# Second block of a transformer kernel: projections from a token-major x that is not yet normed, root and shift applied behind the product

## The chip, the cores and the metric

The kernel runs on one core of a Trainium2 chip. The metric is the device time of the whole program in microseconds, the median of three runs. The engines are named as in the profile: PE is the matmul engine (PEld its weight load), DVE the vector engine, ACT the scalar engine, POOL GpSimd, SP the engine that issues the weight loads.

## The reference

256 tokens of width 1024 go through a first block of two layers (sparse attention, short convolution, gated mix, MLP) and then through a second block, which the change is about:

```python
x = rmsnorm(x, norm_final)                       # end of the first block
ada = silu(c) @ w_ada + b_ada                    # shift1, scale1, gate1, ...
h = rms_norm(x, norm1_g) * (1 + scale1) + shift1
qa, ka, va, qb, kb, vb = split(h @ w_in)         # 512, 128, 128, 512, 512, 512 columns
o_a = windowed_gqa(qa, ka, va)                   # 8 heads, bias and sink
o_b = neighbourhood_attention(qb, kb, vb)        # 8 heads, bias
x = x + gate1 * (concat(rms_norm(o_a), rms_norm(o_b)) @ w_out)
x = x + gate2 * peer(rms_norm(x, norm2_g) * (1 + scale2) + shift2)
return rms_norm(x, final_g)
```

## The kernel before

**Pieces.** All weights come as one stream of 544 pieces of 128 x 1024 floats into a ring of four slots. Each piece is split into a high part (ACT, `split_hi`, L185) and the rest (DVE, `split_lo`, L190), and each product is three matmuls (`mm3`, L213 to L215: high by high, high by low, low by high). `next_piece` (L197) issues the split of the piece three ahead and then makes PE wait for the split of its own. `piece_b` (L217) turns one piece into one tile of 128 outputs by 256 tokens with 24 matmuls of 256 columns. `piece_a` (L242) has the activations as the standing operand, with 12 matmuls of 512 columns per piece.

**Queues.** Every engine works through its instructions in the order in which the Python text issues them. `VE.go`, `AC.go` and `PE.done` (L79 to L90) tie them with semaphores. An instruction that waits holds up all behind it on its engine. Line L88 in the profile is the helper that records nearly all DVE and ACT operations of the two attention blocks.

**The seam into the second block.** The last MLP of the first block ends with three `down` pieces that are held back (`held_pieces`, L337): for each of the four accumulator banks (two token tiles by two halves of the width) all three pieces run in a row, so that the banks end one after another. Behind each, `sum_of` (L1198) adds the bank to x, multiplies by the final gain into `xn`, and ACT takes squares of both. After the last bank PE runs 25 filling matmuls (`keep_clock`, L1221), while DVE makes sums, mean and root (`root`, L292) and two diagonal matrices that hold each token's root. Then `modulated_to_u` (L1153) multiplies `xn` by the diagonals on PE (L1169), which turns it to feature-major and scales it at once; ACT and DVE add scale and shift and split it into `u_hi` and `u_lo`.

**The projections.** `project` (L1374) is a generator of 18 steps over 18 pieces: ka and the first qa tile together (`two_pieces`, L229), the other qa tiles, va, then kb and qb in turn, four times, and last vb, whose four pieces use `piece_a` and so come out token-major. Everything is evicted by ACT alone (`evicted`, L1369). The loop at L1446 runs the steps, and a table written by hand, `beside`, says which attention units take one step behind which projection step. A unit (`unit`, L1254) is one token tile of one attention: a generator whose steps are scores of heads on PE with their bias added on DVE (two steps, the second ends with a maximum over the row on DVE), exponentials on ACT (two steps of four heads), transposes of the probabilities (two steps, evicted by ACT and DVE), the product with v, the scaling by the branch's gain, the transposes into `mx_hi` and `mx_lo`. Units a0 and a1 are the windowed attention, b0 and b1 the neighbourhood one. `masked` (a mask added to the bias of b, steps 0 to 3), `root(st2, ...)` (step 4) and `own_scale` (the norm that x itself gets, steps 5 and 6) are DVE work put between.

Of the kernel before, what the change touches and what calls it, by code (L numbers as in the profile page):

```python
# [49 lines left out]
U_SHIFT, U_REST = 56, 8  # L50
# [43 lines left out]
def build(nc, stream, x_in, gains2, gain_cols, conv_w, w_ada, b_ada, c_cols, kept_in, rope_in, na_mask_in,  # L94
          t5_in, t5_hot, rpb_pad, sinks, sub_keys, gain_out, out):
    ctx = ExitStack()
    with ctx:
# [17 lines left out]
        u_hi = sb(ctx, "u_hi", [P, KD, T], F32R)  # L115
        u_lo = sb(ctx, "u_lo", [P, KD, T], F32R)
# [100 lines left out]
        def piece_b(o, rhs_hi, rhs_lo, kt=KD, parts=1, last=False, ready=None):  # L217

            s = next_piece(last)
            for part in range(parts):  # L220
                for k in range(kt):
# [3 lines left out]
                    i = mm3(o[part], w_hi[:, s, col:col + P], w_lo[:, s, col:col + P],  # L225
                            rhs_hi[:, k, :], rhs_lo[:, k, :], k == 0, k == kt - 1)
            return used(i)
# [288 lines left out]
        gcol = sb(ph1, "gcol", [P, 2, KD])  # L516
# [134 lines left out]
        for layer in range(LAYERS):  # L651
# [409 lines left out]
            if layer < LAYERS - 1:  # L1061
                down(1, tile0 + KH - 3, False)
# [5 lines left out]
            last_tiles = [(a_hi, a_lo, 1), (o_hi, o_lo, 0), (o_hi, o_lo, 1)]  # L1068
            if layer < LAYERS - 1:
                last_tiles.pop(0)  # L1070
            last_downs = (len(last_tiles), lambda j, tt: [a[:, last_tiles[j][2], tt * P:(tt + 1) * P] for a in last_tiles[j][0:2]],
                          acc)
# [20 lines left out]
        og, junk = sb(ph1b, "og", [P, 2, W]), sb(ph1b, "junk", [P, 2, W])  # L1093

# [57 lines left out]

        def modulated_to_u(src, marks, scaled, j, on_act):  # L1153
# [40 lines left out]
        space_lo = [space[:, 0, 0:512], space[:, 2, 0:512]]  # L1194
        scaled = column_scale(0, ada_norm1)
        x_marks, g_marks = [[None, None], [None, None]], [[None, None], [None, None]]

        def sum_of(tt, n):  # L1198
            cols = slice(n * 512, (n + 1) * 512)
            x_marks[tt][n] = add_chunk(x, tt, n, mlp_scale)  # L1200
            g_marks[tt][n] = VE.go((x_marks[tt][n], (s_gain2, 32)), V.tensor_tensor, xn[:, tt, cols],
                                   x[:, tt, cols], gains_b[:, 0, cols], ALU.mult)

        def sums():
            for tt in range(NT):
                for n in range(2):
                    sum_of(tt, n)
                    square_of(x, 5, x_marks, tt, n)
                    if tt + n < NT:
                        square_of(xn, 7, g_marks, tt, n)  # L1210
                    yield

        def square_of(src, row, marks, tt, n):
            cols = slice(n * 512, (n + 1) * 512)
            junk_mark[0] = AC.go((marks[tt][n], junk_mark[0]), S.activation, space_lo[0], src[:, tt, cols], ACT.Square,
                                 accum_out=st[:, row + n, tt:tt + 1])
            return junk_mark[0]

        splits = held_pieces(*last_downs, sums())
        take(5)  # L1220
        keep_clock(5, 25)  # L1221
        m = VE.go((g_marks[1][1],), V.scalar_tensor_tensor, space_lo[1], xn[:, 1, 512:], 1.0, xn[:, 1, 512:],
                  ALU.mult, ALU.mult, accum_out=st[:, 8, 1:2])
        VE.wait(m, junk_mark[0])
        m1 = VE.go((m,), V.tensor_tensor, st[:, 0, :], st[:, 5, :], st[:, 6, :], ALU.add)
        m = VE.go((m,), V.tensor_tensor, st[:, 9, :], st[:, 7, :], st[:, 8, :], ALU.add)
        m1 = VE.go((m1,), V.tensor_scalar, st2[:, 1, :], st[:, 0, :], 1.0 / D, EPS, ALU.mult, ALU.add)
# [854 lines left out]
```

## Time and profile before

| what | value |
|---|---|
| runs | 1728.52 us median of 3 (1727.76 to 1728.98) |
| profiled execution | 1727.02 us, its span 1725.7 us |
| PE, PEld busy | 1700.7 us (99%), 1567.1 us (91%) |
| DVE, ACT busy | 1328.3 us (77%), 926.5 us (54%) |
| granted PE clock | 0.997 over the span |
| weight stream | 544 loads of 512 KB, 3.3 us from issue to landing |

A busy PE in this table is a PE with a matmul in its pipeline; the modelled length of one matmul overlaps the next, so the distance between starts says more than the busy time. Times in the timelines are microseconds from the start of the span, and a row with xN merges N instructions in a row.

### The profile page before, as it was taken

How to read it: one execution, taken by the hardware profiler on the slowest of the kernel's cores; microseconds unless marked ns; L12 is line 12 of the kernel's file. 1: busy time of each engine (PE TensorE's matmuls, PEld its weight loads, DVE VectorE, ACT ScalarE, POOL GpSimd, SP SyncE). 2: the span in 40 equal slices, each digit the busy share in tenths (PEclk: the TensorE clock that was granted, in tenths of full speed). 3: DMA queues.
4: the chain of work that ended last, by engine and by line, in shares of the span. 5: the costliest groups of instructions: out<-in, count | busy, mean ns of one | idle time of the engine just before them, and what ended most of it. 6: DMA issues, size and time to landing. Idle time of an engine off the chain costs nothing.

```text
span 1725.7 us, 33390 instructions
## 1 busy us (share of the span) xinstructions
PE 1700.7 (99%) x11670; PEld 1567.1 (91%) x11670; DVE 1328.3 (77%) x2382; ACT 926.5 (54%) x1647; POOL 63.3 (4%) x112
## 2 busy tenths in 40 slices
PE   9999999999999999999999999999999999999997
PEld 8899899989999899999889999999999988888886
DVE  7986778778976788877775999978888766666666
ACT  5454544455454544455554555577777655444553
POOL 0000001000000122100000000000000000000000
PEclk9999999999999999999999999999999999999999
DMA  6555687755445699744344555554444455555554
GB/s 233 174 187 205 209 294 270 250 174 171 159 160 168 221 329 327 238 153 140 123 167 152 173 170 179 182 171 141 141 138 144 141 191 193 194 194 194 191 192 152
DMA packets 90122, 327.30 MB, mean 190 GB/s; under 512 B 11000, under 2 KB 11176, under 8 KB 89584
## 3 DMA queue, kind: packets, MB, share of 16 engines
q1 hardware_dynamic: 79056, 286.45, 48.8%
q0 software_dynamic: 9712, 34.36, 6.0%
q10 hardware_dynamic: 1264, 5.24, 0.8%
q8 instruction: 62, 1.02, 0.2%
q14 instruction: 28, 0.23, 0.0%
HBM read 323.88 MB, written 6.09 MB: 191 GB/s over the span
## 4 chain that ended last, share of the span: by engine, by line
PE 80%; DVE 16%; issue 2%; ACT 1%; DMA 0%; DVEq 0%; ACTq 0%
PE bank L213 24%; PE bank L215 24%; PE bank L214 24%; DVE Z L88 6%; DVE w_lo L190 5%; PE bank L1772 3%; PE bank L284 1%; DVE yc L88 1%; PE bank L276 1%; PE bank L1313 1%; PE bank L484 1%; DVE work L88 1%; DVE rot L88 1%; DVE top L88 1%; PE bank L1264 0%
## 5 line engine op out<-in xcount | busy, mean ns | idle before, releaser
L190 DVE TENSOR_TENSOR w_lo<-raw,w_hi 128x1024 fp32r<-128x1024 f32 x544 | 658.0, 1220 | 154.1 <-ACT w_hi L185 153.3
L185 ACT ACTIVATE w_hi<-raw 128x1024 fp32r<-128x1024 f32 x544 | 572.5, 1054 | 229.2 <-PE bank L215 162.4
L213 PE MATMUL bank<-u_hi,w_hi 128*128 128x256 f32 x2400 | 686.2, 286 | 3.7 <-DVE w_lo L190 3.0
L214 PE MATMUL bank<-u_lo,w_hi 128*128 128x256 f32 x2400 | 674.7, 281 | 0.0
L215 PE MATMUL bank<-u_hi,w_lo 128*128 128x256 f32 x2400 | 674.7, 281 | 0.0
L213 PEld LDWEIGHTS bank<-u_hi,w_hi 128*128 128x128 f32 x2400 | 453.0, 189 | 12.8 <-DVE w_lo L190 4.3
L214 PEld LDWEIGHTS bank<-u_lo,w_hi 128*128 128x128 f32 x2400 | 453.2, 189 | 2.3
L215 PEld LDWEIGHTS bank<-u_hi,w_lo 128*128 128x128 f32 x2400 | 452.9, 189 | 0.0
L215 PE MATMUL bank<-w_hi,a_lo 128*128 128x512 f32 x744 | 290.6, 391 | 0.0
L214 PE MATMUL bank<-w_lo,a_hi 128*128 128x512 f32 x744 | 290.4, 390 | 0.0
L213 PE MATMUL bank<-w_hi,a_hi 128*128 128x512 f32 x744 | 289.9, 390 | 0.0
L215 PEld LDWEIGHTS bank<-w_hi,a_lo 128*128 128x128 f32 x744 | 139.6, 188 | 29.4
L213 PEld LDWEIGHTS bank<-w_hi,a_hi 128*128 128x128 f32 x744 | 139.9, 188 | 27.9 <-issue 0.2
L214 PEld LDWEIGHTS bank<-w_lo,a_hi 128*128 128x128 f32 x744 | 139.6, 188 | 28.1
L1861 ACT ACTIVATE a_hi<-Z 128x256 fp32r (+1 forms) x126 | 52.7, 418 | 169.0 <-PE bank L215 167.2
L1863 DVE TENSOR_TENSOR a_lo<-Z,a_hi 128x256 fp32r<-128x256 f32 x126 | 53.6, 425 | 81.6 <-ACT a_hi L1861 81.6
L1761 ACT ACTIVATE rows_a<-rows_a,sel 128x128 f32<-128x128 f32 x256 | 81.2, 391 | 0.0
L1745 DVE TENSOR_TENSOR rows_a<-kept,sel 128x512 f32<-128x512 f32 x64 | 44.2, 691 | 34.5 <-PE bank L1772 34.5
L962 ACT ACTIVATE qT<-bank 128x256 f32<-128x256 f32 x64 | 24.6, 384 | 82.5 <-PE bank L215 82.3
L1608 ACT ACTIVATE Z<-bank 128x256 f32 (+1 forms) x68 | 26.1, 384 | 76.8 <-PE bank L215 76.7
L971 DVE CAST a_hi<-qT 128x256 fp32r<-128x256 f32 x60 | 18.1, 301 | 48.4 <-PE bank L215 47.3
L997 DVE SCALAR_TENSOR_TENSOR space<-gate,c_tmp,space 128x1024 f32 x42 | 53.7, 1280 | 0.4
(286 smaller groups left out, 1710.6 us busy)
## 6 DMA issues: line engine op xcount, KB each, us to landing
raw<-stream SPq DMA_DIRECT2D x544, 512.0 KB, 3.3
gate<-w_ada POOLq DMA_DIRECT2D x48, 512.0 KB, 6.0
t_rows<-t_by_distance POOLq DMA_DIRECT2D x8, 256.0 KB, 3.1
rpb_rows<-rpb_pad POOLq DMA_DIRECT2D x8, 224.0 KB, 4.1
bias_b<-rpb_rows POOLq DMA_DIRECT2D x16, 96.0 KB, 6.3
bias_a<-t_rows POOLq DMA_DIRECT2D x1, 1536.0 KB, 13.1
x<-x_in ACTq DMA_DIRECT2D x2, 512.0 KB, 5.5
gains_b<-gains POOLq DMA_DIRECT2D x1, 1024.0 KB, 8.7
```

The costliest lines, as they stand in the source:

```text
L88: return self.done(method(*args, **kw))
L185: nc.scalar.activation(w_hi[:, s, :], raw[:, s, :], ACT.Copy).then_inc(s_hi, 1)
L190: nc.vector.tensor_tensor(w_lo[:, s, :], raw[:, s, :], w_hi[:, s, :].bitcast(F32), ALU.subtract).then_inc(s_split, 1)
L213: M.matmul(o, lh, rh, start=start, stop=False, skip_group_check=True)
L214: M.matmul(o, lh, rl, start=False, stop=False, skip_group_check=True)
L215: return M.matmul(o, ll, rh, start=False, stop=stop, skip_group_check=True)
L997: nc.vector.scalar_tensor_tensor(total, ada_raw[:, k % ADA_RING, :], c_act[:, k:k + 1], total, ALU.mult, ALU.add).then_inc(s_ada, 1)
L1745: return V.tensor_tensor(out, iota.unsqueeze(1).to_broadcast([P, GROUP, P]), values.unsqueeze(2).to_broadcast([P, GROUP, P]), ALU.is_equal)
L1761: i = S.activation(rows_a[:, q, e, :], rows_a[:, q, e, :], ACT.Copy, scale=share[:, e:e + 1])
L1772: i = M.matmul(bank[6 + q][:, e * P:(e + 1) * P], rows_a[:, q, e, :], rows_b[q][:, e, :].bitcast(F32), start=True, stop=True, skip_group_c ...
L1861: S.activation(hi[:, q, :], zj, ACT.Copy).then_inc(s_ah, 1)
L1863: V.tensor_tensor(lo[:, q, :], zj, hi[:, q, :].bitcast(F32), ALU.subtract).then_inc(s_al, 1)
```

## The change

- The held `down` pieces of the last layer are two, as in the first layer; the third runs before them as a piece of its own.
- Behind them x is transposed as it is (16 transposes, two tiles of features to a bank, banks 4 to 7), and ACT and DVE scale it by one gain per feature, which now holds norm_final, norm1_g and 1 + scale1, and split it into u. No root is in it. The filling matmuls, `xn`, the diagonal product and `modulated_to_u` are gone here.
- u has 272 columns for each tile of features instead of 256. Columns 256 and 257 hold the shift, so each of the 18 products has 258 columns, and column 256 of the result is what the shift adds to that output.
- ACT squares x into buffers that are kept; DVE multiplies two tensors of these (four operations over 128x512) for the second mean; `two_roots` follows at step 1, and `roots_as_row` at step 4 makes a 128x256 tile with each token's root in its column.
- Each projection leaves its bank by `rooted_and_shifted`: ACT copies column 256, DVE multiplies the bank by the row of roots, ACT adds the copied column. The first three wait for the row and are issued at step 4, the next three at step 5.
- vb is projected feature-major as the rest and transposed afterwards (`turned_vb`, 8 transposes and two copies behind the first `w_out` piece).
- Units a0 and a1 begin at steps 5 and 6 instead of 3 and 4. `masked` moves to steps 8 to 11, `root(st2)` to step 10, `own_scale` to steps 14 and 15.

```diff
-U_SHIFT, U_REST = 56, 8
+U_SHIFT, U_REST = 8, 8
+U_WIDE = T + 16
...
-            last_tiles = [(a_hi, a_lo, 1), (o_hi, o_lo, 0), (o_hi, o_lo, 1)]
+            last_downs = (2, lambda j, tt: [a[:, j, tt * P:(tt + 1) * P] for a in (o_hi, o_lo)], acc)
...
+        LOWER_ORDER = (0, 2, 1, 3, 4, 6, 5, 7)
+        def lower_scaled(k, hi, lo, j, scaled, turned):
+            b, col = turn_place(k)
+            src, gain, t = bank[b][:, col:col + T], acol[:, 2 * j + 1, k:k + 1], turned[k | 1]
+            m1 = AC.go((t, scaled, *(free[b] if k % 2 else ())), S.activation, hi[:, k, 0:T], src, ACT.Copy, scale=gain)
+            m = VE.go((m1, t, scaled), V.scalar_tensor_tensor, lo[:, k, 0:T], src, gain, hi[:, k, 0:T].bitcast(F32),
+                      ALU.mult, ALU.subtract)
...
+        def roots_as_row(b):
+            take(b)
+            PE.wait(got["diag", 0], got["diag", 1])
+            for tt in range(NT):
+                i = M.matmul(bank[b][:, tt * P:(tt + 1) * P], one[:, 0:1].to_broadcast([P, P]), diag[:, tt, :],
+                             start=True, stop=True, skip_group_check=True)
+            m = AC.go((PE.done(i),), S.activation, token_row[:, :], bank[b][:, 0:T], ACT.Copy)
...
+        def rooted_and_shifted(b, dst, n, done, row):
+            m1 = AC.go((done,), S.activation, side_sum[:, n:n + 1], bank[b][:, T:T + 1], ACT.Copy)
+            m = VE.go((done, row, m1), V.tensor_tensor, dst, bank[b][:, 0:T], token_row[:, :], ALU.mult)
+            free[b] = (m, m1)
+            return AC.go((m, m1), S.activation, dst, dst, ACT.Identity, bias=side_sum[:, n:n + 1])
...
         splits = held_pieces(*last_downs, sums())
-        take(5)
-        keep_clock(5, 25)
...
-        diagonals(root(st, NT, m))
-        split_hi(splits[0]), split_hi(splits[1])
-        split_lo(splits[0])
-        h_ready = modulated_to_u(xn, g_marks, scaled, 0, 0)
-        split_lo(splits[1])
+        for k in range(4, KD):
+            turn_tile(k, 0, x_marks, turned)
+        for k in range(KD):
+            turn_tile(k, 1, x_marks, turned)
+        h_ready = {k: lower_scaled(k, wide_hi, wide_lo, 0, scaled, turned) for k in LOWER_ORDER}
+        for c in splits:
+            split(c)
+        squares_kept(1)
+        for tt in range(NT):
+            for n in range(2):
+                sq = squared[:, 2 * tt + n, :]
+                m = VE.go((square_marks[tt, n],), V.scalar_tensor_tensor, sq, sq, 1.0,
+                          gain_squares[:, n * 512:(n + 1) * 512], ALU.mult, ALU.mult,
+                          accum_out=st[:, 7 + n, tt:tt + 1])
...
         def project():
+            def product(b, ready=None):
+                take(b)
+                return piece_b([bank[b][:, 0:T + 2]], *RAW, ready=ready, order=LOWER_ORDER if ready else None)
+            PE.wait(*shifts)
+            first = [(0, kaT[:, :], "ka", product(0, h_ready))]
             yield
             for f in range(KW):
+                first.append((1 + f, qT[:, f, :], ("qa", f // 2 * 2), product(1 + f)))
+                if f == KW - 1:
+                    row = roots_as_row(7)
+                    for b, dst, name, m in first[0:3]:
+                        got[name] = rooted_and_shifted(b, dst, b, m, row)
+                yield
+            m = product(5)
+            for b, dst, name, done in (*first[3:], (5, vaT[:, :], "va", m)):
+                got[name] = rooted_and_shifted(b, dst, b, done, row)
             yield
+            for f in range(KW):
+                m = product(4)
+                got["kb", f] = rooted_and_shifted(4, kT[:, f, :], 6 + 2 * f, m, row)
+                yield
+                m = product(5)
+                got["qb", f] = rooted_and_shifted(5, qbT[:, f, :], 7 + 2 * f, m, row)
+                yield
+            for f in range(KW):
+                m = product(4 + f % 2)
+                got["vT"] = rooted_and_shifted(4 + f % 2, vT[:, f, :], 14 + f, m, row)
+                yield
...
-        beside = {3: (a0,), 4: (a1,), 5: (a0,), 6: (a1, a0), 7: (a0, a1), 8: (a1,), 9: (a0,),
+        beside = {5: (a0,), 6: (a1, a0), 7: (a0, a1), 8: (a0, a1), 9: (a1, a0),
                   10: (a1, a0), 11: (a1, a0), 12: (a1, b0), 13: (a0, a1), 14: (a0, a1, b0), 15: (b1, b0),
                   16: (b1,), 17: (b0, b1)}
         for n, _ in enumerate(main):
+            if n == 1:
+                mean_mark = two_roots(m)
             if n == 6:
                 turned_va()
-            if n < 4:
-                masked(n)
-            if n == 4:
+            if 8 <= n < 12:
+                masked(n - 8)
+            if n == 10:
                 r1_mark = root(st2, NT, mean_mark)
-            if n in (5, 6):
-                own_scale(n - 5, r1_mark)
+            if n in (14, 15):
+                own_scale(n - 14, r1_mark)
...
             used(i)
+            if k == 0:
+                turned_vb()
             for u in side:
                 next(u)
```

## Rows read from the trace of the kernel before

**Rows 1.** Part 4 of the page: the chain that ended last, shares of the span by engine.

```profile
PE 80%; DVE 16%; issue 2%; ACT 1%; DMA 0%; DVEq 0%; ACTq 0%
```

**Rows 2.** Windows: stretch, us; busy us of PE, PEld, DVE, ACT, POOL; granted clock; DMA.

```profile
775.00:801.00 26.00, 26.00 (x212) 23.98 (x211) 25.61 (x45) 13.11 (x33) 0.00 (x0) 1.00 0.45 146
...
801.00:842.00 41.00, 40.10 (x286) 34.88 (x285) 28.26 (x49) 20.86 (x47) 0.00 (x0) 1.00 0.37 127
```

**Rows 3.** Timeline of PE at the seam: start us, length us, engine, line, operation.

```profile
758.73 5.62 PE L276 MATMUL bank<-one_r 128*128 128x512 f32 x25
...
764.19 3.73 PE L1169 MATMUL bank<-space,xn 128*128 128x128 f32 x32
...
767.68 0.36 PE L213 MATMUL bank<-u_hi,w_hi 128*128 128x256 f32 x1
...
779.21 1.14 PE L1264 MATMUL bank<-kaT,qT 64*128 64x256 f32 x8
```

**Rows 4.** Timeline of PE at the seam between the two layers.

```profile
382.08 0.60 PE L366 MATMUL bank<-kept,x 128*128 128x128 f32 x4
...
383.91 1.77 PE L366 MATMUL bank<-kept,x 128*128 128x128 f32 x12
...
385.44 0.36 PE L213 MATMUL bank<-u_hi,w_hi 128*128 128x256 f32 x1
...
388.58 0.28 PE L213 MATMUL bank<-u_hi,w_hi 128*128 128x256 f32 x1
```

**Rows 5.** Timeline of DVE at the seam into the second MLP.

```profile
575.54 3.22 DVE L88 SCALAR_TENSOR_TENSOR u_lo<-bank,kept,u_hi 128x256 fp32r<-128x256 f32 x8
```

**Rows 6.** Timeline of DVE in the second block, and one row of its MLP.

```profile
760.43 0.69 DVE L88 SCALAR_TENSOR_TENSOR space<-xn 128x512 f32<-128x512 f32 x1
...
761.17 0.23 DVE L88 TENSOR_TENSOR st<-st 128x2 f32<-128x2 f32 x2
...
764.07 1.22 DVE L190 TENSOR_TENSOR w_lo<-raw,w_hi 128x1024 fp32r<-128x1024 f32 x1
...
777.32 1.21 DVE L190 TENSOR_TENSOR w_lo<-raw,w_hi 128x1024 fp32r<-128x1024 f32 x1
...
778.46 0.95 DVE L88 TENSOR_TENSOR bias_b<-bias_b,na_mask 128x768 f32<-128x768 f32 x1
...
781.33 1.28 DVE L88 SCALAR_TENSOR_TENSOR space<-bank,bias_a 128x512 f32<-128x512 f32 x2
...
790.21 2.29 DVE L88 TENSOR_REDUCE rows<-space 128x8 f32<-128x2048 f32 x1
...
793.02 1.22 DVE L190 TENSOR_TENSOR w_lo<-raw,w_hi 128x1024 fp32r<-128x1024 f32 x1
...
581.32 0.41 DVE L965 TENSOR_TENSOR qT<-qT,bank 128x256 f32<-128x256 f32 x1
```

**Rows 7.** Timeline of ACT in the second block.

```profile
769.75 0.42 ACT L88 ACTIVATE u_hi<-hT 128x256 fp32r<-128x256 f32 x1
...
792.93 0.51 ACT L88 ACTIVATE space<-space,rows 128x256 f32<-128x256 f32 x1 [4.08 <-DVE rows L88]
...
794.92 1.04 ACT L185 ACTIVATE w_hi<-raw 128x1024 fp32r<-128x1024 f32 x1
...
804.63 0.19 ACT L88 ACTIVATE rows<-rows 128x8 f32<-128x8 f32 x1
```

**Rows 8.** Timeline of PE in the second block, where the units' PE work begins.

```profile
801.43 1.03 PE L284 MATMUL bank<-kept,space 128*128 128x128 f32 x8
...
805.14 1.03 PE L284 MATMUL bank<-kept,p 128*128 128x128 f32 x8
...
815.38 0.37 PE L213 MATMUL bank<-u_hi,w_hi 128*128 128x256 f32 x1
...
845.38 1.09 PE L284 MATMUL bank<-kept,space 128*128 128x128 f32 x8 [0.34 <-ACT space L88]
...
852.78 1.04 PE L284 MATMUL bank<-kept,p 128*128 128x128 f32 x8
```

More of the change, by code:

```diff
@@ L215, in mm3, with piece_b @@
             return M.matmul(o, ll, rh, start=False, stop=stop, skip_group_check=True)
-        def piece_b(o, rhs_hi, rhs_lo, kt=KD, parts=1, last=False, ready=None):
+        def piece_b(o, rhs_hi, rhs_lo, kt=KD, parts=1, last=False, ready=None, order=None):
             s = next_piece(last)
+            order = order or tuple(range(kt))
             for part in range(parts):
-                for k in range(kt):
+                for k in order:
                     if ready is not None:
@@ L1204, in sums @@
-        def sums():
[L1205 to L1217, printed above, removed]
@@ new lines, in two_roots @@
+        def two_roots(m):
+            VE.wait(m, junk_mark[0])
+            m1 = VE.go((m,), V.tensor_tensor, st[:, 0, :], st[:, 5, :], st[:, 6, :], ALU.add)
+            m = VE.go((m,), V.tensor_tensor, st[:, 9, :], st[:, 7, :], st[:, 8, :], ALU.add)
+            m1 = VE.go((m1,), V.tensor_scalar, st2[:, 1, :], st[:, 0, :], 1.0 / D, EPS, ALU.mult, ALU.add)
+            m = VE.go((m,), V.tensor_scalar, st[:, 4, :], st[:, 9, :], 1.0 / D, None, ALU.mult)
+            m = VE.go((m, m1), V.scalar_tensor_tensor, st[:, 1, :], st2[:, 1, :], EPS, st[:, 4, :],
+                      ALU.mult, ALU.add)
+            diagonals(root(st, NT, m))
+            return m1
@@ new lines, in turned_va, with turned_vb @@
+            got["vat"] = free[7] = (m,)
+        vT = hT
+        def turned_vb():
+            marks = []
+            for tt in range(NT):
+                b = 4 + tt
+                take(b)
+                PE.wait(got["vT"])
+                for f in range(KW):
+                    i = M.transpose(bank[b][:, f * P:(f + 1) * P], vT[:, f, tt * P:(tt + 1) * P], ident)
+                i = PE.done(i)
+                if tt:
+                    m = VE.go((i,), V.tensor_copy, v_sb[:, tt, :], bank[b][:, :])
+                else:
+                    m = AC.go((i,), S.activation, v_sb[:, tt, :], bank[b][:, :], ACT.Copy)
+                free[b] = (m,)
+                marks.append(m)
+            got["vb"] = tuple(marks)
@@ L1399, in project @@
-                AC.go((m,), S.activation, kT[:, f, :], bank[b][:, 0:T], ACT.Copy)
-                m = AC.go((m,), S.activation, qbT[:, f, :], bank[b][:, T:2 * T], ACT.Copy)
-                free[b] = (m,)
-                got["qb", f] = m
-                yield
-            for g in range(KD // 2):
-                m = piece_a([[bank[4][:, :]], [bank[5][:, :]]], U, (2 * g, 2 * g + 1), 512,
-                            g == 0, g == KD // 2 - 1, (4, 5) if g == 0 else ())
-                if g < KD // 2 - 1:
-                    yield
```

119 lines of the change are left out of this document (57 added, 62 removed).

## The prediction

> **What bounds the kernel now.** I read the chain that ended last first: 80% of it is PE [rows 1], so a stage is worth what it adds to PE's own work plus what PE waits in it. Next the windows from 775 to 842 us: PE keeps a granted clock of 1.00, DVE is busy 25.61 us of 26.00 in the first and 28.26 of 41.00 in the second [rows 2]. DVE runs full while the projections start, and PE feels nothing of it, since splits are issued three pieces ahead. Then PE's timeline at the seam: 5.46 us of filling matmuls from 758.73 us, the diagonal product from 764.19, the first projection matmul at 767.68 [rows 3]. These 8.95 us are what the change is after. Last, the timelines of DVE and ACT, for prices and for the order of their queues [rows 6, 7], and the times at which PE begins the units' work [rows 8].
>
> **The seam.** The seam between the two layers has the new shape already: two held pieces, four transposes ahead of the last bank, twelve behind it. There the four take 0.35 us (382.08, next matmul 382.43), from 383.91 to the first product matmul 385.44 are 1.53 us, and the first product, fed by the lowering, lasts until 388.58, 3.14 us [rows 4]. The new code lowers tile 0 only when tile 1 is transposed, and behind four transposes of tiles 4 to 7: five transposes later, about 0.4 us. So: 758.73 + 0.35 + 1.53 + 0.4 = 761.05 for the first product, 764.2 for its end. Before, the pair began at 767.68, and four pieces of 24 matmuls ran to 779.21 [rows 3], 0.120 us each or, without the gaps between pieces, 0.1185 and 2.84 us a piece; half of the pair ends at 770.5. **Gain 6.3 us at the end of the first product.**
>
> **Small terms on PE.** Two columns more: 25 matmuls of 512 columns take 5.46 us, 0.218 each, those of 256 0.120 [rows 3], so 0.4 ns a column and 0.35 us for 18 x 24 x 2. The row of roots is two full matmuls of 128 columns; 32 records of the diagonal product take 3.49 us [rows 3], four records 0.45. vb by `piece_b` costs about what `piece_a` does, some 0.15 us for four. `turned_vb` is eight transposes, 0.9 us by 0.11 each (12 and the wait fit in 1.53 us [rows 4]). Together +1.85. If nothing waited, the change would give 6.3 - 1.85 = 4.4 us.
>
> **DVE at the start.** Its first lowering starts near 760.4 and eight take 3.22 us [rows 5], to 763.65. Then in the order of the queue: one split at 1.14 (777.32 to 778.46 [rows 6]), ready 765.05; four squares times squared gain at 0.74 (760.43 to 761.17), 768.0; two splits, 770.3; `two_roots` at 2.9 (761.17 to 764.07, the same operations), 773.2; three splits, 776.65. PE without a wait starts products 1 to 4 at 764.2, 767.1, 769.9 and 772.8 and wants the split of product 3 at 769.9, which is there at 769.15: it holds, with 0.8 us. Product 5 (va) starts behind the row, at 776.1. So far all gain is kept.
>
> **The new eviction.** It goes ACT, DVE, ACT, and ACT's next copy stands behind its last add, so a run of them does not overlap. Price of one: 0.19 us for a short ACT operation, 0.41 for a DVE product of 128x256 out of a bank, 0.42 for an ACT operation over 128x256 [rows 6, 7]: 1.0 us on ACT, of which DVE loses the same when it has nothing else ahead. Lower bound 0.4 (perfect overlap, DVE's part alone), upper bound 1.1 (the ACT operation at the 0.51 of an exponential with a bias [rows 7]); I take 1.0, since the code's order excludes the overlap. By "ScalarE: Activation LUTs" of the Trainium skill (section on what happens when an exp ACTIVATE runs) a per-partition bias adds about 93 ns to an ACTIVATE, which would put the last step near 0.49 us, the walk below some 0.9 us later and the sum at 1739.5. By that rule; the exponential with its bias, 0.51 us over the same 256 elements [rows 7], agrees.
>
> **What queues behind it.** The three evictions of step 4 run on ACT from 776.7 to 779.75. The first unit's scores need them: PE waits 0.9 us at 779. ACT's `split_hi` (1.0, 794.92 [rows 7]) and DVE's split follow, to 781.95, and only then the evictions of step 5, of which the second frees bank 4 at 783.4. kb0 needs bank 4, and PE, done at 780.9, waits 2.5 us more. From 784.3 DVE has the two units' scores and maxima: 1.20 for two heads' pairs (781.33, length 1.28), 2.81 for a maximum with its small operations (790.21 to 793.02), 1.14 a split [rows 6], without a hole until about 799.9. ACT makes the second half of a0's exponentials (2.0 us for four, 792.93 to 794.92 [rows 7]) only behind the eviction of step 8, which waits for DVE's product there, which stands behind a1's maximum and a split. That gives 800.3 + 2.0 = 802.3. PE, at step 9, is there at 798.25 and **waits 4.1 us**; its transposes began at 801.43 before [rows 8], so here the gain is gone (+1.0). a1 is worse: first half to 804.4, `split_hi` to 805.4, DVE's split and product to 806.95, ACT's add to 807.35, second half to 809.4. PE asks at 806.05, waits 3.4 us, and begins a1's transposes at 809.5 against 805.14 [rows 8], +4.4. Step 10 puts a split, a product, a mask (0.95, 778.46 [rows 6]) and the root (an estimate of 1.7: `two_roots` less its sums and diagonals) ahead of the copies that PE's next transposes want, and the first qb piece behind a0's product with v starts at 819.8 against 815.38 [rows 8], still +4.4.
>
> **The second half.** From step 13 DVE has again no hole: the branch's scales 2.0 (a root and its small operations, an estimate from `two_roots`), two og 1.3 and later two mx_lo 1.2 (512 elements each, like the squares' 0.69), a split, a product, `own_scale` 1.2 (1024 elements like a split), scores 1.2 and b0's maximum 2.2 (2.29 at 790.21 [rows 6]), the last done near 841.65. Against before this stretch holds six evictions and two `own_scale` more. PE waits 0.8 us for og, 2.5 us for a bank that b1's first scores hold, and 1.6 us for the last vb tile, then transposes it (0.95). b0's second exponentials stand behind that tile's eviction, and its transposes start at 855.6 against 845.38; b1's at 862.9 against 852.78 [rows 8]: **+10.1 us**. Behind this everything has the old order and the old load, and the shift goes through to the end.
>
> **Sum.** 1727.0 + 10.1 = 1737.1 against the profiled execution, whose time lies 1.5 us under the median; so 1738.6. All other edits I count at nothing: shift columns, squared gains (1.2 us of DVE ahead of the held pieces, beside a piece that PE runs for 2.8 us) and the wider u. `u_hi` and its neighbours move in memory; no row tells a price for that, and no row of before differs between tiles of u, so zero.
>
> **The rivals.** (1) **PE stays the bound.** All waits of the walk close up, because the exponentials come before PE asks. Then -4.4 us: 1724.1. For it: DVE's and ACT's work sums to less than the stage (DVE is idle for 12.7 us of 41 from 801 us on [rows 2]). Against: it would need both units' exponentials 4 us earlier than the queues give. This is the side other than my forecast, and the point where it decides is step 9: exponentials of a0 ready before 798 us. 0.14. (2) **The evictions cost DVE only 0.4 us each.** The first half then comes some 4 to 5 us earlier and meets PE with little loss; the second half, which is DVE's plain sum, still adds 5 to 6. +5: 1733.5. 0.18. (3) **The clock falls.** The waits of 3 to 4 us are the first of this length; before, filling matmuls stood in the one gap that was longer, and the clock was 1.00 throughout [rows 2]. At 1.2 GHz a piece of 2.84 us takes 5.7; twice this, half of it hidden in the next wait, is about +3: 1741.6. 0.12. "TensorE: Matmul & The Clock Gate" of the Trainium skill (Part 1, the clock gate) says that an array left idle is throttled to half its clock until it has been busy again; whether these waits are enough no row here shows. (4) The terms cancel: gain at the seam, waits of 4 to 5 us, nothing to see. 0.08.
>
> **The numbers.** The forecast has 0.48. 0.2% is 3.5 us, about what a measurement of this kernel tells from no change. Slower by more: forecast, most of (2), and (3), 0.74. Within: (4) and the fast edge of (2), 0.12. Faster: (1), 0.14. The range runs from the fast rival to the slow one with the bounds of the eviction: 1723.5 to 1743.0. The likeliest case's own range is 1735 to 1742.
>
> **What would show it.** Right: first projection matmul near 761 us; a wait of PE for bank 4 at step 6; transposes of L284 behind a wait for ACT at steps 9 and 10, each 3 to 4 us; DVE busy above 85% from 784 to 853; b0's transposes near 855.6. Wrong: transposes of a0 at 798 without a wait, and w_out pieces starting before 842.08; then (1). A first product later than 762 would show that the seam was misread. A granted clock under 1.00 behind the waits would be (3).

## The result and the profile after

| | before | after |
|---|---|---|
| median of the runs | 1728.75 us (4 runs) | 1759.8 us (4 runs) |
| ratio | | 1.0181 [1.0169, 1.0194] |
| profiled span | 1725.7 us | 1759.0 us |
| granted PE clock over the span | 0.997 | 0.992 |

Slower, as forecast, but by 31 us in place of some 10, and outside the range. The chain that ended last is mostly PE's as before ([rows 1]); PE's share fell from 80% to 78%, and those of DVE and ACT each grew by one point:

```profile
PE 78%; DVE 17%; issue 2%; ACT 2%; DMA 0%; DVEq 0%; ACTq 0%
```

The same windows as [rows 2], then the long one that the prediction names (DVE above 85%), then five short ones. The columns are as there; the figure behind POOL is the granted clock.

```profile
775.00:801.00 26.00, 22.45 (x169) 20.79 (x168) 19.02 (x42) 9.39 (x21) 0.00 (x0) 0.93 0.41 139
801.00:842.00 41.00, 33.59 (x266) 31.95 (x264) 27.53 (x67) 22.41 (x63) 0.00 (x0) 0.96 0.27 91
784.00:853.00 69.00, 56.64 (x427) 52.24 (x428) 50.69 (x98) 32.99 (x89) 0.00 (x0) 0.95 0.26 88
788.00:792.00 4.00, 3.58 (x17) 3.58 (x18) 2.97 (x5) 2.02 (x4) 0.00 (x0) 0.57 0.41 135
806.00:812.00 6.00, 2.54 (x12) 2.55 (x13) 2.13 (x5) 5.07 (x19) 0.00 (x0) 0.75 0.27 87
850.00:856.00 6.00, 4.34 (x20) 3.24 (x20) 4.90 (x8) 3.51 (x12) 0.00 (x0) 0.78 0.26 87
856.00:862.00 6.00, 6.00 (x30) 5.72 (x30) 4.97 (x5) 2.21 (x5) 0.00 (x0) 0.65 0.28 92
862.00:875.00 13.00, 10.41 (x49) 8.47 (x48) 5.19 (x7) 9.73 (x29) 0.00 (x0) 0.87 0.33 120
```

PE loses 3.55 us of the first window and 7.41 of the second, DVE is less busy than before in the first (19.02 against 25.61), and the clock, 1.00 before, falls to 0.57 in one stretch. From 784 to 853 us DVE is busy 50.69 of 69 us, 73%. No engine is full: this is a stage of engines that wait for each other.

Timeline of PE in the changed kernel. L1161 transposes x, L215 to L217 are the three matmuls of a product, L1331 scores, L287 the units' transposes. In brackets stands the idle time ahead of a row and who ended it.

```profile
762.75 0.39 PE L217 MATMUL bank<-w_hi,o_lo 128*128 128x512 f32 x1
762.98 1.66 PE L1161 MATMUL bank<-kept,x 128*128 128x128 f32 x12
764.97 0.36 PE L215 MATMUL bank<-u_hi,w_hi 128*128 128x258 f32 x1 [0.33 <-DVE u_lo L89]
...
784.84 1.14 PE L1331 MATMUL bank<-kaT,qT 64*128 64x256 f32 x8 [1.12 <-ACT qT L89]
788.42 0.49 PE L215 MATMUL bank<-u_hi,w_hi 128*128 128x258 f32 x1 [2.44 <-DVE qT L89]
...
789.14 0.42 PE L215 MATMUL bank<-u_hi,w_hi 128*128 128x258 f32 x1
789.35 0.42 PE L216 MATMUL bank<-u_lo,w_hi 128*128 128x258 f32 x1
...
809.46 1.97 PE L287 MATMUL bank<-kept,space 128*128 128x128 f32 x8 [3.99 <-ACT space L89]
...
816.58 1.10 PE L287 MATMUL bank<-kept,p 128*128 128x128 f32 x8 [1.76 <-ACT p L89]
...
852.73 2.64 PE L1331 MATMUL bank<-kT,qbT 64*128 64x256 f32 x8 [1.66 <-DVE p L89]
...
867.32 1.12 PE L287 MATMUL bank<-kept,space 128*128 128x128 f32 x4 [2.59 <-ACT v_sb L89]
...
875.72 1.04 PE L287 MATMUL bank<-kept,p 128*128 128x128 f32 x8
...
909.00 0.36 PE L215 MATMUL bank<-u_hi,w_hi 128*128 128x256 f32 x1
```

Three landmarks cut the program: the start of the last held `down` matmul (758.49 us before, 762.75 here), the first product matmul behind the attention block (886.04, 909.00) and the end of the span.

| part | before | after | more |
|---|---|---|---|
| up to the last held matmul | 758.49 | 762.75 | 4.3 |
| attention stage | 127.55 | 146.25 | 18.7 |
| all behind it | 839.66 | 849.99 | 10.3 |

The last part runs no instruction that the change rewrites, and the first only a few at its end, but both are longer. In the last part the same matmuls start a little farther apart. PE in the last phase, first before, then after:

```profile
1500.03 0.39 PE L213 MATMUL bank<-w_hi,a_hi 128*128 128x512 f32 x1
...
1502.75 0.39 PE L213 MATMUL bank<-w_hi,a_hi 128*128 128x512 f32 x1
```

```profile
1500.09 0.39 PE L215 MATMUL bank<-w_hi,a_hi 128*128 128x512 f32 x1
...
1502.89 0.39 PE L215 MATMUL bank<-w_hi,a_hi 128*128 128x512 f32 x1
```

Twelve matmuls of the same size take 2.72 us in one and 2.80 in the other; the length shown for one is 0.39 in these rows, so only the starts tell it. The distance from the start of one matmul to the start of the next is called the step below. Its means over 1400 to 1700 us are 0.2267 and 0.2333 us. Behind the stage stand 3 x 504 such matmuls: 1512 x 0.0066 = 10.0 of the 10.3 us. The first part is less certain: kernels with the same instructions and the same layout up to there (s_dve_moved and s_dve_moved_bank6, below) reach that landmark at 758.07 and 761.00 us, so differences of up to 3 us between single profiles mean little there.

### The profile page after: what moved, and what is told of

The parts are those of the page before. It is cut to its first block, busy times and chain, and to the rows that moved or that the text cites. A ratio compares the mean times of both kernels' runs of the same rounds, so it can differ in the third digit from the quotient of the medians.

```text
span 1759.0 us, 33500 instructions
## 1 busy us (share of the span) xinstructions
PE 1721.9 (98%) x11689; PEld 1577.9 (90%) x11689; DVE 1335.1 (76%) x2402; ACT 930.0 (53%) x1662; POOL 63.5 (4%) x112
## 4 chain that ended last, share of the span: by engine, by line
PE 78%; DVE 17%; issue 2%; ACT 2%; DMA 0%; DVEq 0%; ACTq 0%
PE bank L215 24%; PE bank L217 23%; PE bank L216 23%; DVE Z L89 6%; DVE w_lo L192 5%; PE bank L1847 3%; DVE yc L89 1%; PE bank L1380 1%; PE bank L287 1%; PE bank L487 1%; DVE work L89 1%; DVE rot L89 1%; PE bank L279 1%; DVE top L89 1%; DVE rows L89 0%
## 5 line engine op out<-in xcount | busy, mean ns | idle before, releaser
L215 PE MATMUL bank<-u_hi,w_hi 128*128 128x256 f32 (+1 forms) x2432 | 699.3, 288 | 5.3 <-DVE qT L89 2.4
L216 PE MATMUL bank<-u_lo,w_hi 128*128 128x256 f32 (+1 forms) x2432 | 687.8, 283 | 0.0
L217 PE MATMUL bank<-u_hi,w_lo 128*128 128x256 f32 (+1 forms) x2432 | 684.8, 282 | 0.0
L215 PEld LDWEIGHTS bank<-u_hi,w_hi 128*128 128x128 f32 x2432 | 460.4, 189 | 16.2 <-issue 4.3
L216 PEld LDWEIGHTS bank<-u_lo,w_hi 128*128 128x128 f32 x2432 | 461.4, 190 | 2.8
L217 PEld LDWEIGHTS bank<-u_hi,w_lo 128*128 128x128 f32 x2432 | 463.5, 191 | 0.0
L217 PE MATMUL bank<-w_hi,a_lo 128*128 128x512 f32 x744 | 294.1, 395 | 0.0
L215 PE MATMUL bank<-w_hi,a_hi 128*128 128x512 f32 x744 | 293.8, 395 | 0.0
L217 PEld LDWEIGHTS bank<-w_hi,a_lo 128*128 128x128 f32 x744 | 139.7, 188 | 33.6
L215 PEld LDWEIGHTS bank<-w_hi,a_hi 128*128 128x128 f32 x744 | 139.7, 188 | 31.4 <-issue 0.2
```

The source lines that it names most:

```text
L215: M.matmul(o, lh, rh, start=start, stop=False, skip_group_check=True)
L216: M.matmul(o, lh, rl, start=False, stop=False, skip_group_check=True)
L217: return M.matmul(o, ll, rh, start=False, stop=stop, skip_group_check=True)
```

## The experiments

### Does the place in memory alone cost it?

Two theories: either the tiles behind u were moved in memory, and this has a price by itself; or the last phase pays for something that the change does. Edits: **before_new_places** is the kernel before with the changed kernel's layout, **before_rest_216** moves a_hi and all behind it but leaves u, **after_old_places** is the changed kernel with a_hi at its old address, **after_shift_56** the changed kernel with 48 more columns ahead of u.

```diff
# before_new_places: U_SHIFT, U_REST = 8, 8; tiles of u 272 columns wide, 256 used
# before_rest_216
-U_SHIFT, U_REST = 56, 8
+U_SHIFT, U_REST = 56, 216
# after_old_places
-U_SHIFT, U_REST = 8, 8
-U_WIDE = T + 16
+U_SHIFT, U_REST = 24, 8
+U_WIDE = T + 2
# after_shift_56
-U_SHIFT, U_REST = 8, 8
+U_SHIFT, U_REST = 56, 8
```

> The kernel before with nothing but the change's layout of memory: u with 272 columns in a row of which 256 are used, 8 floats of gap ahead of it. No instruction is added or dropped. Theory of places (where u, a and all behind them lie sets how fast matmuls follow each other): the 14 us that the changed kernel loses outside the second block's attention stage (3.9 ahead of 760 us, 10.3 behind 909 us) appear here, 1743 us (1741 to 1745), with a start-to-start of 0.2333 us instead of 0.2267 for 512-column matmuls in the last phase. Rival (the loss comes with the instructions of the change or with slower loads, or is drift between chips): 1728 to 1730 us.

> The kernel before with u where it was and only the gap behind u grown by 208 floats, so that a_hi, a_lo and all tiles behind lie 832 bytes further, as in the changed kernel. If the place of a and of what lies behind it makes the loss: 1738 to 1742 us, with the 512-column matmuls that load a at 0.2333 us and the 256-column ones that stream u unchanged at 0.1184. If it is the place of u or its longer row: 1728 to 1731 us.

> The changed kernel with 258 columns of u in a row and gaps of 24 and 8 floats, so that a_hi and all behind it lie at the same addresses as in the kernel before; u itself starts 128 bytes earlier than before and has rows of 1032 bytes. Nothing else differs from the changed kernel. Theory of places, with a as the cause: 1759.8 less 10 to 14 = 1746 to 1750 us. If the loss outside the stage came from something else of the change: 1758 to 1761 us.

> The changed kernel with the gap ahead of u back at 56 floats: u_hi starts where it started before, and a_hi and all behind it lie exactly 1024 bytes further than before. Theory of places, if only the address within 1024 bytes counts: the same gain as with the old places, 1746 to 1750 us. If the absolute place or the row of 1088 bytes counts: no gain, 1758 to 1761 us.

| run | median us | ratio to before | 512-column step, us | stage | behind it |
|---|---|---|---|---|---|
| before_new_places | 1741.05 | 1.0073 [1.0056, 1.009] | 0.2333 | 127.6 | 850.2 |
| before_rest_216 | 1740.08 | 1.0069 [1.0052, 1.0086] | 0.2333 | 127.5 | 849.7 |
| after_old_places | 1750.83 | 1.013 [1.0113, 1.0146] | 0.2267 | 146.6 | 841.6 |
| after_shift_56 | 1747.84 | 1.0109 [1.0092, 1.0126] | 0.2267 | 146.6 | 840.3 |

The layout alone makes the kernel before 12.1 us slower than the 1728.95 of its own runs beside it; taking it back makes the changed kernel 9 to 12 us faster than its 1759.8. The attention stage doesn't notice (146.25, 146.6, 146.6): 9 to 12 of the 31 us are the place of a_hi and its followers, and some 19 are the stage. (after_old_places, which gives the 9, also has u at another address and with shorter rows.) The price of the place alone was expected at 10 to 14 us; the rivals, which had no change of time, fell.

### What in the address counts?

Counted up from the tiles ahead of it (each column is 4 bytes of a partition), a_hi starts at 65792 B before (a multiple of 256), at 66624 after, and at 66816, again a multiple of 256, in after_shift_56. Six more versions of the kernel before move u, or a_hi with all behind it, by those two constants alone.

```diff
-U_SHIFT, U_REST = 56, 8
+U_SHIFT, U_REST = 8, 8      # before_u_shift_8: u and a_hi 192 B lower
+U_SHIFT, U_REST = 56, 72    # before_rest_72: a_hi 256 B higher
+U_SHIFT, U_REST = 56, 24    # before_rest_24: a_hi 64 B higher
+U_SHIFT, U_REST = 56, 40    # before_rest_40: a_hi 128 B higher
+U_SHIFT, U_REST = 8, 56     # before_u_alone: u 192 B lower, a_hi in place
+U_SHIFT, U_REST = 32, 32    # before_u_shift_32: u 96 B lower, a_hi in place
```

> The kernel before with 8 columns ahead of u in place of 56: u and every tile behind it lie 192 B lower, a_hi so at 64 modulo 1024 as in the changed kernel, though at another absolute place; nothing else differs. Theory (the step of the matmuls on a_hi's neighbourhood goes by the address modulo 1024 B): 1740 to 1741 us, 512-column matmuls 0.233 us apart in the last phase. Rival (by the absolute place, or by the distance to another tile): 1728 to 1730, 0.2265 us apart.

> The kernel before with 72 spare columns behind u in place of 8: a_hi and every tile behind it 256 B higher, at 512 modulo 1024. No earlier run has this residue. If only some residues are bad and before's is not the best, the 512-column matmuls lie under 0.2260 us apart and the time is 1718 to 1727; if before's residue is one of many good ones, 1728 to 1730; if most residues are bad, 1738 to 1742.

> The kernel before with 24 columns behind u in place of 8: a_hi and what is behind it 64 B higher, 64 modulo 128 as in the changed kernel, at 320 modulo 1024, a residue that no run had. Theory (a_hi is slow wherever it is not a multiple of 128 B): 1738 to 1741 us and 0.233 us apart in the last phase. Rival (slow at 64 modulo 256 alone or modulo 1024 alone; this one is also 64 modulo 256, so only the last is told apart): 1727 to 1730 and 0.2267.

> The kernel before with 40 columns behind u in place of 8: a_hi and what is behind it 128 B higher, a multiple of 128 B and not of 256. If multiples of 128 B are enough: 1727 to 1730 us and 0.2265 to 0.2270 us apart in the last phase; if it has to be a multiple of 256: 1738 to 1741 and 0.233.

> The kernel before with 8 columns ahead of u in place of 56 and 56 behind it in place of 8: u_hi and u_lo lie 192 B lower, a_hi and everything behind it where it was. With everything 192 B lower the time was 1732.0 against the 1740.1 of a_hi alone being moved to the same residue, the projections 0.1164 to 0.1170 us apart in place of 0.1178 to 0.1188. Theory (the two places add up, each by itself): a_hi costs nothing now and u gains 8: 1719 to 1722 us. Rival (what counts is the distance between u and a_hi, or of the pair): 1728 or more.

> The kernel before with 32 columns ahead of u and 32 behind it: u at residue 0 modulo 128 B, a_hi in place. Seen so far: u at 96 modulo 128 takes 0.1178 to 0.1188 us a projection's matmul, at 32 modulo 128 0.1164 to 0.1170. If a residue of 0 is best, as for a_hi: 1715 to 1720; if only the neighbourhood of 32 is good: 1726 to 1730.

The last column is the mean step behind each of the three matmuls of a product that reads u, in the order of the code.

| run | a_hi modulo 256 | u modulo 256 | median us | ratio to before | 512-column step | steps of u's three matmuls, 590 to 740 us |
|---|---|---|---|---|---|---|
| before | 0 | 224 | 1727.7 to 1729.0 | | 0.2267 | 0.1188, 0.1178, 0.1181 |
| before_rest_72 | 0 | 224 | 1728.71 | 1.0003 [0.9994, 1.0013] | 0.2267 | 0.1188, 0.1178, 0.1181 |
| before_rest_24 | 64 | 224 | 1739.42 | 1.0064 [1.0047, 1.0081] | 0.2333 | 0.1183, 0.1185, 0.1184 |
| before_rest_40 | 128 | 224 | 1738.46 | 1.006 [1.0043, 1.0077] | 0.2324 | 0.1184, 0.1183, 0.1183 |
| before_u_shift_8 | 64 | 32 | 1731.97 | 1.0024 [1.0014, 1.0033] | 0.2333 | 0.1164, 0.1169, 0.1170 |
| before_u_alone | 0 | 32 | 1721.03 | 0.9956 [0.994, 0.9973] | 0.2267 | 0.1170, 0.1168, 0.1165 |
| before_u_shift_32 | 0 | 128 | 1731.02 | 1.0018 [1.0008, 1.0028] | 0.2267 | 0.1177, 0.1198, 0.1213 |

PE of before_rest_40, twelve matmuls of the same kind as above, 2.78 us:

```profile
1500.08 0.40 PE L213 MATMUL bank<-w_hi,a_hi 128*128 128x512 f32 x1
...
1502.86 0.40 PE L213 MATMUL bank<-w_hi,a_hi 128*128 128x512 f32 x1
```

Several of my guesses fell here. The modulus is not 1024 (before_rest_72, at another residue of it, is fast) and 128 isn't enough (before_rest_40 is slow): all six layouts with a_hi at a multiple of 256 B have the fast step, all five at 64 or 128 B above one the slow step. And before_u_shift_8 came out between its two theories, since u moved as well. before_u_alone takes the two apart: with a_hi back in place it is 10.9 us under before_u_shift_8, and 7.3 under the kernel before. The places add up, each by itself, as the first theory there said. For u no rule came out. With rows of 1024 B a start at 32 is good, 128 and 224 are not (before_u_shift_32 came out slower than both of its forecasts), and three residues are all that ran. Nor is 32 good by itself: before_new_places has u at 32 too, but with rows of 1088 B, and its steps are 0.1180, 0.1196 and 0.1183.

I moved tiles together and not a single operand, so the runs don't separate a_hi from a tile behind it that moves along. The traces say something on it. Matmuls that stream o_hi, o_lo, y_hi or y_lo, which lie behind a_hi and move with it, went the other way: their steps are 0.1182 to 0.1184 us in the kernel before and 0.1165 to 0.1170 in before_rest_24. The 512-column matmuls that hold u_hi or u_lo have steps of 0.233 to 0.234 us in both. So the slow step is not common to all matmuls, but goes with the tiles that a matmul reads; why, no run tells.

### The clock

All further runs stand on after_shift_56 (1747.84 us, stage 146.6), so that the place is out of the comparison. **s_fill** puts filling matmuls into a free bank at five of the waits, 52 in all.

```diff
+        fills = {(9, a0): (6, 16), (10, a1): (7, 8), (16, b1): (7, 8)}
...
+                if (n, u) in fills:
+                    b, count = fills[n, u]
+                    take(b)
+                    keep_clock(b, count)
...
+            if n == 5:
+                take(6)
+                keep_clock(6, 10)
...
+                take(7)
+                keep_clock(7, 10)
```

> The changed kernel with 56 floats of gap (1747.8 us) plus filling matmuls of 512 columns at five of PE's waits in the second block: 10 behind step 5, 16 ahead of a0's first transposes, 8 ahead of a1's, 8 ahead of b1's second scores, 10 ahead of b0's first transposes. Theory of the clock (the stage is longer than the walk by 9 us because PE falls to the lower of its two levels behind its waits; windows of 0.57 to 0.83): the granted clock stays at 1.00 and the time falls by 4 to 8 us, to 1740 to 1744. Rival (ACT and DVE set the chain also there, the slow matmuls lie beside it): clock 1.00, but 1746 to 1748 us. If the fillers themselves run into the chain: 1749 or more.

1742.81 us (1.008 [1.0063, 1.0097]), 5.0 less. The windows, first of after_shift_56, then of s_fill:

```profile
784.00:791.00 7.00, 5.47 (x25) 5.47 (x26) 3.62 (x7) 2.58 (x6) 0.00 (x0) 0.52 0.30 90
806.00:812.00 6.00, 4.47 (x25) 4.48 (x26) 1.86 (x5) 4.54 (x17) 0.00 (x0) 0.72 0.22 79
...
860.00:875.00 15.00, 11.46 (x59) 9.41 (x58) 6.47 (x9) 10.92 (x30) 0.00 (x0) 0.89 0.40 131
```

```profile
784.00:791.00 7.00, 6.95 (x55) 6.12 (x54) 5.97 (x11) 3.65 (x7) 0.00 (x0) 1.00 0.42 146
806.00:812.00 6.00, 4.62 (x33) 4.04 (x33) 3.32 (x6) 4.43 (x14) 0.00 (x0) 1.00 0.24 87
...
860.00:875.00 15.00, 13.81 (x92) 12.50 (x93) 8.40 (x11) 8.01 (x17) 0.00 (x0) 1.00 0.43 140
```

The granted clock is back at 1.00. The fillers do none of the attention's work; they only stand where PE waited. The stage takes 142.5 us in place of 146.6. So the clock is 4 to 5 of the 19 us, as far as the fillers don't delay anything themselves; some 15 stand without it.

### The eviction

ACT and DVE in the changed kernel, the first evictions of step 4:

```profile
781.17 0.17 ACT L89 ACTIVATE side_sum<-bank 128x1 f32<-128x1 f32 x1
781.93 0.51 ACT L89 ACTIVATE kaT<-kaT,side_sum 128x256 f32<-128x256 f32 x1 [0.59 <-DVE kaT L89]
782.35 0.15 ACT L89 ACTIVATE side_sum<-bank 128x1 f32<-128x1 f32 x1
783.06 0.51 ACT L89 ACTIVATE qT<-qT,side_sum 128x256 f32<-128x256 f32 x1 [0.56 <-DVE qT L89]
```

```profile
781.47 0.42 DVE L89 TENSOR_TENSOR kaT<-bank,token_row 128x256 f32<-128x256 f32 x1 [0.57 <-ACT side_sum L89]
782.60 0.42 DVE L89 TENSOR_TENSOR qT<-bank,token_row 128x256 f32<-128x256 f32 x1 [0.70 <-ACT side_sum L89]
```

One takes 1.13 us (product to product, 781.47 to 782.60). ACT is idle for half of it, and DVE for more than half. Two edits: **s_noshift** leaves the shift out (only DVE's product remains), **s_dve** has the same arithmetic on DVE alone.

```diff
 # s_dve
-            m1 = AC.go((done,), S.activation, side_sum[:, n:n + 1], bank[b][:, T:T + 1], ACT.Copy)
-            m = VE.go((done, row, m1), V.tensor_tensor, dst, bank[b][:, 0:T], token_row[:, :], ALU.mult)
+            m1 = VE.go((done,), V.tensor_copy, side_sum[:, n:n + 1], bank[b][:, T:T + 1])
+            m = VE.go((done, row), V.tensor_tensor, dst, bank[b][:, 0:T], token_row[:, :], ALU.mult)
             free[b] = (m, m1)
-            return AC.go((m, m1), S.activation, dst, dst, ACT.Identity, bias=side_sum[:, n:n + 1])
+            return VE.go((m, m1), V.tensor_scalar, dst, dst, side_sum[:, n:n + 1], None, ALU.add)
```

> The changed kernel with 56 floats of gap, whose eviction of a projection is DVE's product alone: ACT's copy of column 256 and ACT's add of it are left out, so the shift is missing from the result. Theory of the queue (the eviction's path ACT, DVE, ACT makes exponentials late and holds banks): 18 evictions lose 0.6 us of ACT each and all handing over; the transposes of a0 and a1 come 3 to 5 us earlier, the time is 1738 to 1742 us. Rival (DVE's plain sum is the bound): only 1 to 3 us gained, 1745 to 1747.

> The changed kernel with 56 floats of gap, with the whole eviction on DVE: it copies column 256, multiplies by the row and adds the column, ACT does nothing. Theory of the queue: as without the shift, less what 18 times 0.35 us more on DVE cost where DVE has no hole, 1741 to 1745 us. Rival (DVE's plain sum is the bound): slower than 1747.8, up to 1754.

s_noshift: 1730.32 us (1.0003 [0.9993, 1.0012]), stage 128.4. s_dve: 1735.15 (1.0035 [1.0023, 1.0048]), stage 134.1. Both were faster than either of their forecasts. So 17.5 of the 19 us hang on the two ACT operations of each eviction, and 12.7 of these went when the same arithmetic moved to DVE. How much of the 12.7 is the hand-over between engines, how much ACT's freed queue, and how much the shorter operations (an add of 0.35 us in place of 0.51) is not separated. DVE of s_dve:

```profile
778.58 0.15 DVE L89 COPY side_sum<-bank 128x1 f32<-128x1 f32 x1
778.65 0.41 DVE L89 TENSOR_TENSOR qT<-bank,token_row 128x256 f32<-128x256 f32 x1
779.10 0.35 DVE L89 TENSOR_SCALAR qT<-qT,side_sum 128x256 f32<-128x256 f32 x1
779.37 0.15 DVE L89 COPY side_sum<-bank 128x1 f32<-128x1 f32 x1
```

0.79 us an eviction, without a hop from engine to engine; ACT's exponentials no longer stand behind an add that waits for DVE. What PE still waits for are single long operations of DVE, and one of these waits brings the clock down:

```profile
810.72 0.66 PE L287 MATMUL bank<-kept,p 128*128 128x128 f32 x4 [1.40 <-DVE xn L89]
...
841.63 2.38 PE L1331 MATMUL bank<-kT,qbT 64*128 64x256 f32 x8 [2.63 <-DVE p L89]
```

```profile
825.00:850.00 25.00, 21.55 (x138) 18.96 (x137) 23.37 (x48) 11.49 (x31) 0.00 (x0) 0.86 0.25 86
```

### The order of the queue

**s_defer** leaves the eviction on both engines and issues it behind the units' work of its step. **s_dve_moved** is s_dve with the root of the second statistic and both `own_scale` at step 12; **s_dve_moved_bank6** also gives the first kb product another bank.

```diff
 # s_defer
-                got["kb", f] = rooted_and_shifted(4, kT[:, f, :], 6 + 2 * f, m, row)
+                put(("kb", f), 4, kT[:, f, :], 6 + 2 * f, m, row)
...
+            while later:
+                later.pop(0)()
 # s_dve_moved
-            if n == 10:
+            if n == 12:
                 r1_mark = root(st2, NT, mean_mark)
-            if n in (14, 15):
-                own_scale(n - 14, r1_mark)
+                own_scale(0, r1_mark)
+                own_scale(1, r1_mark)
 # s_dve_moved_bank6, besides
+                b = 4 if f else 6
```

> The changed kernel with 56 floats of gap; from step 6 on the eviction of a projection is issued behind the unit steps of its own step instead of ahead of them, the instructions are the same. Theory of the queue: exponentials no longer stand behind an eviction that waits for DVE; PE's waits of 4 and 1.8 us for a0 and a1 shrink by 2 to 4 us in all, 1743 to 1746 us. Rival (DVE's sum): no change, 1747 to 1748, or slower where a bank comes free later.

> The changed kernel with 56 columns ahead of u (a_hi at before's address modulo 1024 B), the whole eviction on VectorE, and the root of the second statistic and both of VectorE's scales of the next block moved behind the sixth product's evictions (step 12). Queue theory (the stage is long because products wait for a bank that stands behind single long pieces of work on VectorE): the 1.40 us wait ahead of the a0 side's transposes and the 2.63 us wait ahead of the a1 side's, with the half clock of 825:850, go from their places, the half clock costing about as much as the waits: 1730 to 1733 us. Rival (the work is only moved, and VectorE has no room in the stage: the waits come back behind step 12): 1734 to 1737, with one wait of over 2 us behind step 12 in place of the two.

> The same, and the first half of kb goes into bank 6, so that its product doesn't wait for bank 4's eviction of qb: the wait of 1.18 us ahead of it goes. Queue theory: 0.8 to 1.2 us less than the run beside it. Rival (bank 6 is taken from the scores, whose start then waits as long): the same time as the run beside it within 0.3 us.

s_defer missed: 1754.03 us (1.0153 [1.0136, 1.017]), 6 us slower than its base. The 4.04 us wait for the exponentials went. Two waits for banks took its place, and one of 6.25 us for the last vb tile, ahead of its transposes (L1444):

```profile
804.82 0.58 PE L215 MATMUL bank<-u_hi,w_hi 128*128 128x258 f32 x1 [4.09 <-DVE qbT L89]
...
850.94 0.39 PE L215 MATMUL bank<-u_hi,w_hi 128*128 128x258 f32 x1 [3.15 <-DVE hT L89]
...
869.65 1.94 PE L1444 MATMUL bank<-kept,hT 128*128 128x128 f32 x8 [6.25 <-ACT hT L89]
```

By the order of the code the evictions now stand behind the units' maximum (DVE's product for qbT starts at 804.35, behind a maximum of 2.29 us). They hold their banks as long as they held the exponentials before: both orders lose. s_dve_moved came out as its theory said, and a little under the range: 1729.35 us (1.0008 [0.9999, 1.0018]), stage 129.2:

```profile
827.87 1.32 PE L287 MATMUL bank<-kept,og 128*128 128x128 f32 x8 [2.39 <-DVE og L89]
...
837.69 1.73 PE L1331 MATMUL bank<-kT,qbT 64*128 64x256 f32 x8 [0.24 <-DVE p L89]
```

```profile
825.00:850.00 25.00, 21.80 (x147) 18.25 (x146) 23.54 (x49) 14.31 (x38) 0.00 (x0) 1.00 0.36 114
```

The rival was half right: a wait of 2.39 us does stand behind step 12. But it takes the place of 4.03 us of two waits and 0.81 of a third, and the clock stays at 1.00 (0.14 of 25 us, 3.5). The other bank brought nothing: 1731.16 (1.0015 [1.0005, 1.0025]). The wait ahead of that product went, the wait ahead of the next kb product grew from 1.17 to 1.66 us, and the stage is 129.2 us in both. The 2.9 us between their profiles ahead of the stage (758.07 and 761.00) come from no edit.

So the change with its eviction on one engine, its long DVE operations moved and its layout at the old residue is as fast as the kernel before, and not faster. The one version that beats both is before_u_alone, the kernel before with its u 192 B lower.

## Why the prediction was right and wrong

- **The seam**: right in itself, though the sign I set for a misread seam (a first product later than 762) fired. Forecast 761.05 us for the first product; 764.97 came, 3.92 later, and the last held matmul ran 3.9 later too (762.75 less 758.49 and the 0.35 of the transposes). From there to the first product are 2.22 us, 2.21 by the forecast. What came late lies ahead of the seam: before_new_places has 2.5 us of it by its layout alone, and single profiles differ by up to 3 us there. The 0.33 us wait for `u_lo` is in the four tenths that I had added.
- **Small terms on PE** and **DVE at the start**: nothing speaks against them; PE has no wait over 0.2 us between 764.97 and 784.84. One sum was off: 763.65 and a split of 1.14 give 764.79, not 765.05. In s_noshift, where all of them stand, the stage is 0.8 us longer than before and not 4.4 shorter, so some 5 us of waits and slower clock remain even with the cheapest eviction; its window from 825 to 850 us has a clock of 0.93.
- **The new eviction**: mechanism right, size a little low: 1.13 us where I took 1.0. The bound of 1.1 was exceeded, because I summed three durations and no time between engines: DVE's product starts 0.25 to 0.30 us after ACT's copy has, ACT's add 0.46 after that, and the next copy 0.42 after that. The add took 0.51, like the exponential with its bias in [rows 7], which was my upper case. The rule I quoted with it ("ScalarE: Activation LUTs" of the Trainium skill, the section on what an ACT_TABLE_LOAD costs) gives 0.49, which the trace's 0.51 bears out better than the 0.42 I took.
- **What queues behind it**: the places were right, one by one: bank 4 at step 6 (2.5 forecast, 2.44), a0's transposes (4.1, 3.99), b1's scores (2.5, 1.66). a1's wait was 1.76 and not 3.4, since PE itself came later. Two were not: the 1.6 us for the last vb tile didn't come, and 2.59 us stood inside b0's transposes (867.32), for a bank whose copy on ACT was issued behind exponentials and a split. These rows look like a hit, and the clock times didn't: with 3.9 us taken off for the later start, a0's transposes came at 805.6 (802.35 forecast, 3.2 late), b1's at 871.8 (862.9, 8.9 late). Waits can agree while PE's work between them grows. And DVE was not full: I forecast it above 85% busy from 784 to 853 us, and it was at 73%. The walk had it without a hole; the trace has it idle for 0.57 to 0.70 us ahead of each product where evictions follow each other (781.47 to 789.07). So "DVE's plain sum" was the wrong picture of the second half; it is the chain through both engines.
- **Rival (3), the clock**, was not a rival but part of the likeliest case: it came on top. In the windows the clock has fallen already behind 1.12 and 2.44 us of waiting (0.57), not only behind the waits of 3 to 4 us, and s_fill puts it at 4 to 5 us, not +3.
- **The second half**: +10.1 was forecast at b1's transposes; without the later start it was +19. 4 to 5 are the clock. The evictions' 0.13 us more, over 18, are 2.3 at most. What is left, some 2 us, I can't put down to one row.
- **Sum, the step that failed most**: "`u_hi` and its neighbours move in memory; no row tells a price for that, and no row of before differs between tiles of u, so zero". It was 9 to 12 us, as much as the whole forecast. That no row told a price was true; zero didn't follow from it. The change touches every address behind u, and those tiles feed thousands of matmuls: 0.0066 us for each of 1512 in the last phase alone is 10 us. An unknown price on so many instructions should have gone into the range with a width of its own, on both sides, since before_u_alone shows 7.3 us to be had the other way. It is not the only step that failed: the forecast with 12 us for the place, 1750.6 us, and the stage without it, 1747.8 (after_shift_56), each lie outside 1743.0 by themselves. In the stage the terms that were too small are the clock (nothing in the sum, 4 to 5 us measured) and the price of an eviction (1.0 for 1.13).
- **Rival (1)**, a faster kernel, didn't come, for the reason given: the exponentials of a0 were ready at 809.3. **Rival (2)** asked for evictions that cost DVE 0.4 only; s_noshift builds that, and shows what it would have been worth (17.5 us against after_shift_56, 1730.3 where I had 1733.5).

## What to carry to other kernels

An eviction that goes from one engine to another and back costs more than its operations, since everything queued behind its last part waits with it: the same arithmetic on one engine gave 12.7 us of 1748, though that was the busier engine. A change of tile sizes moves every tile behind; compare the distance between starts of identical matmuls far from the edit before blaming the edit, and try a gap of a few columns. And when a walk forecasts waits, forecast the clock behind them too.

## What the runs showed of the hardware that I had not expected

- **Addresses.** The distance between matmuls depends on where tiles lie in memory. 512-column matmuls on a_hi were 0.2267 us apart with a_hi at a multiple of 256 B and 0.2324 to 0.2333 with it 64 or 128 B above one, six layouts against five, and those on u (256 columns) 0.1164 to 0.1213 by the place of u. What costs one tile can help another: the shift of 64 B that slowed a_hi took o_hi from 0.1184 to 0.1166. The last phase ran at a granted clock of 1.00 in both kernels. "SBUF — State Buffer" of the Trainium skill (the section on the two separate sides) says that PE's port never waits on anyone. The traces neither confirm nor refute that: whether this is another engine's traffic or the engine's own two reads no run here tells.
- **The clock.** It stood at its lower level (matmuls of 258 columns 0.214 us apart, 789.14 and 789.35, where 0.12 is usual; of the two levels that is 1.2 GHz) behind a wait of 1.12 us, eight short matmuls and a wait of 2.44 us. A single wait of 2.39 us in s_dve_moved, with no wait over 0.36 us in the 20 us ahead of it, left it at 1.00.
